# Dilated attention of a three-layer transformer kernel: the order in which eight query tiles are worked on

## Chip, cores and metric

One core of one Trainium2 chip (trn2). The metric is the device time of one execution in microseconds (us), the median of three runs. The profile is of one execution of its own.

## What is computed

The reference runs three layers over 1024 tokens of width 1024 in float32 and returns one array of 1 x 1024 x 1024. The third layer holds the part that matters here: an attention of 8 heads of 64 columns in which a query attends to earlier tokens under three patterns of strides, mixed by their softmax sums.

```
DILATED_CONFIGS = ((128, 1), (512, 4), (2048, 16))      # window, dilation
for window, dilation in DILATED_CONFIGS:
    o, lse = dilated_window_attention(qh, kh, vh, window, dilation)
wts = softmax(stack(lses), axis=0)
o = sum(wts[..., None] * stack(outs), axis=0)           # then * silu(gate)
```

The mixture equals one causal softmax in which each key counts as often as patterns reach it. The kernel computes it so: it adds the logarithm of that count (times 8, or a large negative number where no pattern reaches the key) to the scores, from one table `mask_dilated`.

## The kernel before, in words

The kernel is written out by hand, one instruction stream per engine (TensorE, VectorE, ScalarE, GpSimd, SyncE), joined by semaphores. A planner builds a list of stages once, and each engine's function walks that list. The dilated attention is the stage `att_dil`, kind "dilated"; ahead of it are projections (q, k with their norms, v), behind it the stage "ssm".

The work of the stage is a list of 32 pairs, built at lines 967 to 978: for each query tile `t` of 128 queries (0 to 7) and each head pair `hp` (0 to 3) one pair. Query tile `t` sees the key tiles 0 to `t`, so its score rows are `(t + 1) * 128` keys wide: 128 for tile 0, 1024 for tile 7. `full_pieces` cuts the width into pieces of at most 512 keys, so tiles 0 to 3 have one piece and tiles 4 to 7 two. The two heads of a pair are its two lanes.

`plan_pairs` (line 595) numbers everything in the order of the list: the pair's position `at`, its block (one block per query tile), the PSUM banks of its scores and turned probabilities, and its chunks. A pair's probabilities, `2 * (t + 1)` tiles of 128 x 128 in all, are turned in one chunk (tiles 0 to 3, up to 8 tiles) or in two (tiles 4 to 7: the last 8 in the second one). The score pieces and the first of two chunks take banks in turn from the ring `main` (5 banks), the last chunk of each pair from the ring `turn` (2 banks). A chunk is turned as two halves of 64 rows, one copied out of PSUM by ScalarE and the other by VectorE.

The four loops over the list, one step of each for pair `i` (`u`):

- TensorE (lines 2151 to 2166): scores of pair i+1 (L1705), values of pair i-1 (L2115), turning of pair i (L2087, which waits for both lanes' exponentials of i). Values wait for the chunk's two copies and for the output of the pair before, since all pairs share the PSUM bank of the outputs. After the last pair its values come on their own, then one transpose of the sums (L2170).
- VectorE (lines 3305 to 3323): minima of pair i+1, for each piece both lanes (L3223: adds the mask, scales, stores to SBUF and keeps the minimum), then its half of the copies of pair i (L3237).
- ScalarE (lines 3800 to 3817): exponential of pair i+1, lane 0 (L3718), output of pair i-1 (L3772), its half of the copies of pair i (L3730), exponential of pair i+1, lane 1 (L3718). An exponential works on the whole width of a lane at once and waits for the last minimum of its lane.
- GpSimd (lines 1442 to 1470): when the last pair of a query tile has its output, it stores the tile's block of 128 x 512 to `y_dil` (L1460). Two SBUF blocks alternate (`pair_block`), so a block's first output waits for the store of two blocks before. At the end the inverted sums are stored (L1466), and the stage "ssm" starts its loads (L1542 and on).

Score rows live in one of three SBUF slots per lane (`pair_slot`, by `at % 3`). Sums and outputs are addressed by `t` and `hp`, not by the position in the list. Two further attentions of the kernel use the same loops: the grid attention (2 or 3 local key tiles and 2 of the context, ends at about 1518 us) and, with a loop of its own, the latent attention (1280 keys, starts at about 1034 us).

Of the kernel before, what the change touches and what calls it, by code (L numbers as in the profile page):

```python
# [114 lines left out]
def build(nc, io, out):  # L115
    x, ctx_in = io["x"][0], io["ctx"][0]
    ctx = ExitStack()
    with ctx:
# [651 lines left out]
        with_ctx, tokens = list(range(NTC)), list(range(NT))  # L770
# [42 lines left out]
        def full_pieces(k0, w):  # L813
            return [{"at": at, "k0": k0 + at, "w": min(512, w - at), "add": None} for at in range(0, w, 512)]
# [150 lines left out]
            q["rows"]["after"] = (q["rows"]["ready"] - 1) % 2  # L965
        mask_dilated = RM[:, 0:1024]
        pairs = []
        for t in tokens:
            for hp in range(4):
                w, m0 = (t + 1) * P, (7 - t) * P  # L970
                pieces = full_pieces(0, w)
                for pc in pieces:
                    pc["add"] = mask_dilated[:, m0 + pc["at"]:m0 + pc["at"] + pc["w"]]
                pairs.append({"t": t, "hp": hp, "first": hp == 0, "last": hp == 3, "pieces": pieces,
                              "key_tiles": list(range(t + 1)),
                              "qk": [[(qT[64 * a:64 * a + 64, hp, t * P:(t + 1) * P], kT[64 * a:64 * a + 64, hp, :])
                                      for a in range(2)]],
                              "v": vl, "vc": [128 * hp, 128 * hp + 64], "y": 128 * hp, "to": y_dil[:, :, t * P:(t + 1) * P]})
# [2924 lines left out]
```

How the kernel before makes its waits and increments, by code:

```python
    def wait_full(self, eng, f):  # L100
        eng.wait_ge(self.full, f + 1)
# [1 line left out]
    def wait_drained(self, eng, f):  # L104
        eng.wait_ge(self.drained[self.side[f]], self.count[f])
# [1 line left out]
    def written(self, ins):  # L108
        ins.then_inc(self.full, 1)
# [214 lines left out]
        def wait_weights(eng, n):  # L324
            eng.wait_ge(s_w[weights[n]["slot"]], 16 * weights[n]["loads"] * (weights[n]["nth"] + 1))
# [755 lines left out]
        def wait_x(eng, i):  # L1081
            eng.wait_ge(s_x[i % 4], 16 * (i // 4 + 1))
# [184 lines left out]
        @block.sync  # L1268
        def _(sp):
            row = lambda ap, n: ap.rearrange("(a n) -> a n", a=1).broadcast_to([P, n])
            for n in range(n_weights):
                w = weights[n]
                if w["before"] is not None:
                    (early if w["before"] in even_cols["w"] else main).wait_full(sp, weights[w["before"]]["last"])
                if n == even_rows["w"][0]:
                    sp.wait_ge(s_xn, last_norm + 1)
                    sp.dma_start(bada_row[0], row(io["ev_b_ada"][0][2048:3072], 1024)).then_inc(s_bada, 16)
                if n == odd_rows["w"][0]:
                    main.wait_drained(sp, last_window_scores)
# [16 lines left out]
                j = ple["tiles"][i]  # L1296
                half = slice(512 * c, 512 * c + 512)
                sp.wait_ge(s_ple, n + 1)
                sp.dma_start(out[0, j["t"] * P:(j["t"] + 1) * P, half], x_slot(j["x"])[:, half]).then_inc(s_final[i % 4], 16)
            for r in range(4):
                sp.wait_ge(s_final[r], 32 * len(range(r, len(ple["tiles"]), 4)))
```

## Time and profile before

| | |
|---|---|
| median of 3 runs | 2467.17 us (2466.59 to 2469.29) |
| the profiled execution | 2466.88 us |
| its span, first to last instruction | 2465.1 us |
| instructions | 39768 |
| TensorE matmul busy | 2431.7 us (99%) |
| TensorE weight load busy | 1811.3 us (73%) |
| VectorE busy | 1493.4 us (61%) |
| ScalarE busy | 789.8 us (32%) |
| GpSimd busy | 302.0 us (12%) |
| granted TensorE clock, mean | 1.000 |

The span is the profiled time from the first to the last instruction; 1.8 us lie around it. Busy times of TensorE are those of overlapping matmuls with modelled ends, so a group's duration can reach a little into the next group; from the start of one group to the start of the next is the surer measure. "<-" at an idle time names what ended it.

### The profile page before, as it was taken

What the parts mean: (1) busy time and instruction counts of PE and PEld (TensorE: products, weight loads), DVE (VectorE), ACT (ScalarE), POOL (GpSimd) and SP (SyncE); (2) the same over time, 40 slices, a digit from 0 to 9 for tenths busy, and PEclk for the clock granted to TensorE, in tenths of its full rate; (3) what the DMA queues carried; (4) which work ended last, traced back from release to release, by engine and by line L of the source; (5) the groups of instructions that cost most, each with busy time, mean ns of one, the idle gap of its engine ahead of it and who ended that gap; (6) DMA issues with size and microseconds to landing.
All of it is one profiled execution on the core that took longest, in us unless ns stands there. A gap on an engine that the chain in (4) does not pass through costs nothing.

```text
span 2465.1 us, 39768 instructions
## 1 busy us (share of the span) xinstructions
PE 2431.7 (99%) x15379; PEld 1811.3 (73%) x15379; DVE 1493.4 (61%) x3624; ACT 789.8 (32%) x1849; POOL 302.0 (12%) x491
## 2 busy tenths in 40 slices
PE   9999999999999999999999999999999999999999
PEld 4577688777788785577788776868578775546867
DVE  3268776699776664444452487767778683425454
ACT  3247410377711123333300075112312373221211
POOL 2001000000051000000060042310000004132100
PEclk9999999999999999999999999999999999999999
DMA  8130010122032220311011013432241206244421
GB/s 300 43 108 24 19 35 35 43 75 78 18 119 96 89 91 30 107 44 43 14 24 40 34 60 37 123 108 99 90 150 35 78 19 166 98 139 151 154 77 51
DMA packets 79498, 193.74 MB, mean 79 GB/s; under 512 B 7948, under 2 KB 18896, under 8 KB 78272
## 3 DMA queue, kind: packets, MB, share of 16 engines
q0 software_dynamic: 28928, 99.67, 12.9%
q1 hardware_dynamic: 49632, 91.17, 10.7%
q8 instruction: 123, 2.02, 0.3%
q14 instruction: 63, 0.52, 0.1%
q10 hardware_dynamic: 752, 0.38, 0.1%
HBM read 149.46 MB, written 42.07 MB: 78 GB/s over the span
## 4 chain that ended last, share of the span: by engine, by line
PE 95%; DVE 2%; ACT 1%; issue 1%; DMA 1%; DVEq 0%; SPq 0%; POOL 0%; ACTq 0%
PE psum L1672 38%; PE psum L1705 12%; PE psum L2007 8%; PE psum L2118 6%; PE psum L2115 5%; PE psum L2199 4%; PE psum L2087 4%; PE psum L1811 3%; PE psum L1928 3%; PE psum L1658 1%; PE psum L1639 1%; PE psum L2273 1%; PE psum L2291 1%; PE psum L2257 1%; PE psum L1980 1%
## 5 line engine op out<-in xcount | busy, mean ns | idle before, releaser
L3718 ACT ACTIVATE RP<-RP,small 128x1280 f32<-128x1280 f32 (+10 forms) x272 | 250.4, 923 | 183.4 <-DVE small L3223 183.0
L1705 PE MATMUL psum<-RQ 64*128 64x256 f32 (+5 forms) x1344 | 287.7, 488 | 1.7 <-ACT RQ L3460 0.8
L3223 DVE CUSTOM_DVE_ANT_0 RP<-psum,small 128x512 f32<-128x512 f32 (+1 forms) x370 | 197.2, 571 | 58.9 <-PE psum L1705 54.8
L2007 PE MATMUL psum<-RW,hT 128*128 128x512 f32 (+3 forms) x608 | 217.1, 512 | 1.0 <-ACT hT L3426 1.0
L1705 PEld LDWEIGHTS psum<-RQ 64*128 64x128 f32 (+1 forms) x1344 | 147.4, 188 | 82.3 <-issue 55.1
L2007 PEld LDWEIGHTS psum<-RW,hT 128*128 128x128 f32 x608 | 128.8, 217 | 75.4 <-issue 57.8
L1672 PE MATMUL psum<-RW,hT 128*128 128x256 f32 x736 | 167.1, 379 | 0.0
L1672 PEld LDWEIGHTS psum<-RW,hT 128*128 128x128 f32 x736 | 139.7, 190 | 22.2 <-issue 2.1
L1672 PE MATMUL psum<-RW,RP 128*128 128x256 f32 x576 | 136.2, 379 | 0.0
L2115 PEld LDWEIGHTS psum<-RP,RQ 128*64 128x64 f32 x1856 | 100.3, 137 | 46.2 <-issue 30.4
L2115 PE MATMUL psum<-RP,RQ 128*64 128x128 f32 x1856 | 124.5, 278 | 7.8 <-DVE RP L3237 4.2
L2118 PE MATMUL psum<-RQ,RP 128*128 128x128 f32 x1024 | 125.5, 279 | 0.8 <-DVE RP L3245 0.8
L2087 PEld LDWEIGHTS psum<-ident,RP 64*128 64x128 f32 x2668 | 97.0, 139 | 39.0 <-issue 27.1
L2118 PEld LDWEIGHTS psum<-RQ,RP 128*128 128x128 f32 x1024 | 119.2, 192 | 4.1 <-DVE YR L3279 0.9
L2087 PE MATMUL psum<-ident,RP 64*128 64x64 f32 x2668 | 112.4, 227 | 6.3 <-ACT RP L3718 5.5
L1672 PEld LDWEIGHTS psum<-RW,RP 128*128 128x128 f32 x576 | 107.7, 190 | 13.4
L3237 DVE COPY RP<-psum 128x512 f32<-128x512 f32 (+3 forms) x168 | 87.6, 525 | 35.8 <-PE psum L2087 33.3
L1672 PE MATMUL psum<-RW,RQ 128*128 128x256 f32 x480 | 108.9, 379 | 0.0
L1672 PEld LDWEIGHTS psum<-RW,RQ 128*128 128x128 f32 x480 | 90.5, 190 | 12.6 <-issue 1.0
L1672 PE MATMUL psum<-RQ,RP 128*128 128x256 f32 x432 | 97.2, 380 | 0.9 <-issue 0.9
L1672 PEld LDWEIGHTS psum<-RQ,RP 128*128 128x128 f32 x432 | 81.6, 190 | 11.9 <-issue 1.3
L1811 PE MATMUL psum<-RW,hT 128*128 128x512 f32 x160 | 73.7, 595 | 0.6 <-DVE hT L2562 0.6
(574 smaller groups left out, 4249.7 us busy)
## 6 DMA issues: line engine op xcount, KB each, us to landing
RW<-in_w_in SPq DMA_DIRECT2D x7, 2048.0 KB, 7.9
RW<-in_od_w_ada SPq DMA_DIRECT2D x6, 2048.0 KB, 8.2
RW<-in_ev_w_in SPq DMA_DIRECT2D x5, 2048.0 KB, 7.9
RW<-in_od_w_in SPq DMA_DIRECT2D x5, 2048.0 KB, 7.8
RQ<-in_ev_w_ada SPq DMA_DIRECT2D x8, 1024.0 KB, 14.9
RX<-in_x POOLq DMA_DIRECT2D x12, 512.0 KB, 7.4
RW<-in_ev_w_ada SPq DMA_DIRECT2D x2, 2048.0 KB, 8.6
RW<-in_ev_w_out SPq DMA_DIRECT2D x2, 2048.0 KB, 9.0
```

What stands on the lines that cost most here:

```text
L1672: last = pe.matmul(main.bank(f)[:, 0:256], lhs(i), rhs[:, i, :], start=i == 0, stop=i == 3)
L1705: last = pe.matmul(ring.bank(f)[:, 0:pc["w"]], q, kk[:, keys], start=i == 0, stop=i == len(u["qk"]) - 1)
L1811: return pe.matmul(main.bank(j["m"]), lhs_of("h", j["t"], kk), w_buf(n)[:, kk, :], start=kk == 0, stop=kk == KC - 1)
L1928: last = pe.matmul(main.bank(f), yT[kk], w_buf(st["w"][c])[:, kk, :], start=kk == 0, stop=kk == KC - 1)
L2007: last = pe.matmul(main.bank(f)[:, c0:c0 + nc_], lhs_of(st["lhs"], j["t"], kk), w, start=kk == 0, stop=kk == kn - 1)
L2087: last = pe.transpose(ring.bank(f)[:, HD * i:HD * i + HD], pair_slot(st, u, lane)[rows, at:at + P], ident[rows, rows])
L2115: last = pe.matmul(bank_o[64 * lane:64 * lane + 64, 0:P], u["v"][:, kt, vc:vc + 64], p_t, start=first, stop=final)
L2118: last = pe.matmul(bank_o[:, P * lane:P * lane + P], p_t, u["v"][:, kt, vc:vc + P], start=first, stop=final)
L2199: last = pe.matmul(main.bank(e["m"]), *pair, start=kk == 0, stop=kk == KC - 1)
L3223: drained(ring, dve.tensor_tensor_reduce(pair_slot(st, u, lane)[:, pc["at"]:pc["at"] + pc["w"]], ring.bank(f)[:, 0:pc["w"]], add, -scale, ...
L3237: drained(ring, dve.tensor_copy(turned_half(ch, 1), src), f)
L3718: fn(pr, pr, ACT.Exp, bias=mins[:, at, lane, n - 1:n], scale=-1.0, accum_out=total).then_inc(s_pexp, 1)
```

## The change

The list of pairs is built over the query tiles in another order. The head pairs inside a tile, and everything that is computed for a pair, stay as they are.

```diff
@@ -965,7 +965,7 @@
             q["rows"]["after"] = (q["rows"]["ready"] - 1) % 2
         mask_dilated = RM[:, 0:1024]
         pairs = []
-        for t in tokens:
+        for t in (5, 0, 6, 1, 7, 2, 4, 3):
             for hp in range(4):
                 w, m0 = (t + 1) * P, (7 - t) * P
                 pieces = full_pieces(0, w)
```

`tokens` is 0 to 7. All engines take the new order, since all walk the same list.

## Rows read from the trace of the kernel before

**Rows 1.** The page: engines' share of the span, and the chain by engine

```profile
PE 2431.7 (99%) x15379; PEld 1811.3 (73%) x15379; DVE 1493.4 (61%) x3624; ACT 789.8 (32%) x1849; POOL 302.0 (12%) x491
...
PE 95%; DVE 2%; ACT 1%; issue 1%; DMA 1%; DVEq 0%; SPq 0%; POOL 0%; ACTq 0%
```

**Rows 2.** Busy time by stretch: length, engines (instructions), clock, DMA share, GB/s

```profile
1951.86:2049.40 97.54, 93.34 (x1345) 66.64 (x1345) 77.12 (x242) 75.36 (x207) 5.00 (x7) 1.00 0.13 43
...
1958.50:1965.50 7.00, 6.36 (x76) 3.73 (x76) 4.93 (x20) 6.13 (x26) 0.74 (x1) 1.00 0.21 66
...
2031.00:2049.50 18.50, 17.71 (x303) 14.20 (x302) 12.98 (x33) 12.24 (x26) 0.71 (x1) 1.00 0.06 17
```

**Rows 3.** Timeline of the stage's first steps, tile 0: start, duration, what, [idle before]

```profile
1951.86 0.71 PE L1705 MATMUL psum<-RQ 64*128 64x128 f32 x8
...
1953.25 0.39 ACT L3718 ACTIVATE RP<-RP,small 128x128 f32<-128x128 f32 x1
...
1953.78 0.34 PE L2087 MATMUL psum<-ident,RP 64*128 64x64 f32 x4 [1.21 <-ACT RP L3718]
...
1956.55 0.26 ACT L3772 ACTIVATE YR<-psum 128x128 f32<-128x128 f32 x1
...
1956.70 0.27 ACT L3730 ACTIVATE RP<-psum 128x128 f32<-128x128 f32 x1
...
1956.86 0.40 ACT L3718 ACTIVATE RP<-RP,small 128x128 f32<-128x128 f32 x1
```

**Rows 4.** Timeline, TensorE's gaps where the next tile is one longer

```profile
1958.73 0.44 PE L2115 MATMUL psum<-RP,RQ 128*64 128x128 f32 x4 [0.42 <-ACT RP L3730]
...
1965.69 0.66 PE L2115 MATMUL psum<-RP,RQ 128*64 128x128 f32 x8 [0.30 <-ACT RP L3730]
...
1985.60 1.10 PE L2115 MATMUL psum<-RP,RQ 128*64 128x128 f32 x16 [0.41 <-issue]
```

**Rows 5.** Timeline, TensorE's gaps at the stage's end, tile 7

```profile
2043.98 1.97 PE L2115 MATMUL psum<-RP,RQ 128*64 128x128 f32 x32 [0.39 <-DVE RP L3237]
...
2047.50 1.97 PE L2115 MATMUL psum<-RP,RQ 128*64 128x128 f32 x32 [0.40 <-DVE RP L3237]
```

**Rows 6.** Timeline, TensorE: one step of tile 5, then scores of 6 and 7

```profile
2004.53 1.51 PE L1705 MATMUL psum<-RQ 64*128 64x512 f32 x8
...
2005.96 1.53 PE L2115 MATMUL psum<-RP,RQ 128*64 128x128 f32 x24
...
2007.42 0.96 PE L2087 MATMUL psum<-ident,RP 64*128 64x64 f32 x24
...
2008.22 1.72 PE L1705 MATMUL psum<-RQ 64*128 64x512 f32 x8
...
2029.18 1.93 PE L1705 MATMUL psum<-RQ 64*128 64x512 f32 x8
```

**Rows 7.** Timeline, first exponentials of tiles 4 (with its scores), 5, 6 and 7

```profile
1987.30 1.30 PE L1705 MATMUL psum<-RQ 64*128 64x512 f32 x8
...
1990.14 0.83 ACT L3718 ACTIVATE RP<-RP,small 128x640 f32<-128x640 f32 x1 [0.86 <-DVE small L3223]
...
2007.50 0.94 ACT L3718 ACTIVATE RX<-RX,small 128x768 f32<-128x768 f32 x1 [0.84 <-DVE small L3223]
...
2011.33 1.05 ACT L3718 ACTIVATE RP<-RP,small 128x896 f32<-128x896 f32 x1 [0.97 <-DVE small L3223]
...
2032.42 1.15 ACT L3718 ACTIVATE RX<-RX,small 128x1024 f32<-128x1024 f32 x1 [1.08 <-DVE small L3223]
```

**Rows 8.** Timeline of other attentions: latent, first turning; grid, last values

```profile
1040.23 0.71 PE L2087 MATMUL psum<-ident,RP 64*128 64x64 f32 x16 [1.99 <-ACT RP L3718]
...
1517.23 1.09 PE L2115 MATMUL psum<-RP,RQ 128*64 128x128 f32 x16 [0.91 <-DVE RP L3237]
```

**Rows 9.** DMA issues of 1940 to 2080 us: KB each, median us to landing

```profile
y_dil<-YR POOLq DMA_DIRECT2D x8, 256.0 KB, 2.7
```

**Rows 10.** Busy time by stretch around the latent attention's start, clock third from last

```profile
1036.00:1060.00 24.00, 21.38 (x170) 14.56 (x169) 11.51 (x34) 8.42 (x14) 0.00 (x0) 1.00 0.28 102
```

## The prediction, made before the change was run

> **What bounds the kernel now.** I read the page first: TensorE is busy for 99% of the span and makes up 95% of the chain of waits that ended last [rows 1], so a change is worth what it adds to or takes from TensorE's path. Next the stretches: the dilated attention lasts 97.5 us, 4.0% of the span, with TensorE busy for 93.34 us of it, VectorE for 77.12 and ScalarE for 75.36 [rows 2]. TensorE still ends most waits, but in the short tiles it is not full (6.36 of 7.00 us), and in the last stretch it isn't either. Then the timeline, where the gaps lie: 1.21 us before the first turning, small ones at the short tiles and on the way into tile 4, two at the end [rows 3 to 5].
>
> **How one step is built.** Every engine walks the same list of 32 pairs (8 tiles, 4 head pairs). In step i TensorE computes the scores of pair i+1, then the values of pair i-1, then turns (transposes) pair i. VectorE runs the masked minima of i+1 and then half of the copies of i. ScalarE runs the exponential of i+1's lane 0, the output of i-1, its half of the copies of i, the exponential of i+1's lane 1. So between the scores of a pair and its turning stand only the values and the turning of the two pairs before it. With neighbours of like length these cover the minima and exponentials; with a short pair ahead of a long one they don't.
>
> **What is removed or added: nothing.** The same 32 pairs with the same widths run on each engine: no instruction, byte or DMA more. Only seams between tiles and both ends of the stage change. Before, the seams go up by one tile seven times. After, they go down four times (5 to 0, 6 to 1, 7 to 2, 4 to 3) and up three times by a lot (0 to 6, 1 to 7, 2 to 4); the stage starts with tile 5 instead of 0 and ends with 3 instead of 7.
>
> **Prices, start to start.** In tile 5 scores take 1.43 us (2004.53 to 2005.96), values 1.46, turning 0.80 [rows 6]. A tile of 128 keys more or less is 0.21 in scores (1.93 against 1.51 over two tiles), 0.22 in values (1.97 against 1.53) and 0.13 in turning (0.96 against 0.34 over five) [rows 3, 5, 6]. Four steps of each of the eight tiles make 91.7 us, against 97.5 measured: 5.8 us of stall, 4.2 of it visible as gaps [rows 2], the rest as stretched groups of scores or values. The other half of a seam is how late the first exponential comes after the start of the scores: 2.84 us in tile 4, 2.97 in tile 5, 3.11 in tile 6, 3.24 in tile 7; one then lasts 0.83, 0.94, 1.05 and 1.15 us [rows 6, 7]. On ScalarE an output takes 0.15 us and the copy of a pair of tile 0 0.16 (1956.55, 1956.70, 1956.86) [rows 3]; a tile more adds 0.1 to a copy, as it does to an exponential. The turning follows the end of the second by 0.14 (1953.25 plus 0.39, then 1953.78) [rows 3].
>
> **The start.** Tile 5: first exponential at 2.97, two of 0.94, turning at 5.0 us. TensorE has two scores of 1.43 to do meanwhile, 2.86 us: it stalls 2.1. Tile 0 stalls 1.21 [rows 3]. Extra 0.9. Bounds: nothing extra, and 1.3 (a cold start twice as wide, with 1280 keys, idles 1.99 [rows 8]; 2.1 is already beyond it, and 0.4 is for a slower bank).
>
> **5, 0, 6.** Going down, the values of the last pair of tile 5 come right behind 0.37 us of scores, where 1.43 covered its copies: about 0.2, and the turning before it waits 0.35 for its lane 1 exponential (which in a row of tile 5 pairs has 1.43 us of scores ahead of it, here 0.37). Inside tile 0 the steps stay bound by the handing back and forth, as now. Going up, count from the start of the scores of the first pair of tile 6. Its exponential starts at 3.11 and ends at 4.16; behind it on ScalarE stand the output of the pair before last and the copy of the last pair of tile 0, until 4.5; then lane 1 until 5.5, turning at 5.65. TensorE has scores 1.66, values 0.37, turning 0.17, scores 1.66, so it is through at 3.9; the last values of tile 0 can start at 4.65 (a stall of 0.8), end at 5.0, and the turning waits 0.65 more. With the 0.6 that two steps of tile 0 lose inside, this makes 2.6 us. Tile 0 and its way into tile 1 lose 1.3 today (gaps like the 0.42 ahead of the last of them [rows 4], and stretched groups). Extra 1.3.
>
> **6, 1, 7.** Same walk: exponential at 3.24 to 4.4, output and copy to 4.8, lane 1 to 5.95, turning at 6.1; TensorE is through with scores 1.86, values 0.59, turning 0.29, scores 1.86 at 4.6: 0.35, then 0.55; inside tile 1 0.45, a bank 0.15. 1.5 against 0.8 today. Extra 0.7.
>
> **7, 2, 4, 3.** Exponential at 2.84 to 3.7, output and copy to 4.2, lane 1 to 5.0; TensorE is through at 3.7: 0.65; inside tile 2 0.25. 0.9 against 0.4. Extra 0.5. On the other side the seam from 3 to 4, now a gap of 0.41 and a little stretch [rows 4], and a part of tile 4's stretched groups go: minus 0.65 together.
>
> **The end.** The last two values wait for copies with no scores in between. Tile 7's pairs are turned in two chunks, the first is copied while the second is turned: 0.39 and 0.40 us [rows 5]. A pair of tile 3 is one chunk of 16 transposes, and the grid attention ends with exactly such a pair: 0.91 [rows 8]. Twice 0.91 less 0.79: extra 1.0, the firmest term.
>
> **What costs nothing.** The block stores land 2.7 us after issue [rows 9], and their buffer is wanted again two tiles later; the shortest tile in between lasts over 4 us (four steps of 0.9 and their stalls). If that cover were gone, the price would be 2.7 once. The next stage starts from the end of this one whatever the tile, so a delay passes on in full.
>
> **Sum.** 0.9 + 1.3 + 0.7 + 0.5 - 0.65 + 1.0 = 3.75, taken as 3.8 us. Bounds: if the three upward seams cost no more than now, the sum is 1.3 (0.9, -0.65, 1.0); if each costs as much as the cold start (2.1), it is 7.1. I take the walked value, since its durations are rows of this stage and its end is a row of a like stage. The profiled execution took 2466.88 us, 0.3 below the median of 2467.17: it would take 2470.7, the median 2471.0. About 0.2%, 4.9 us, is what a measurement can tell from no change.
>
> **Rivals.**
>
> *The seams cost as much as the start (slower).* Place: ScalarE's queue at the three upward seams. The long exponential stands ahead of an output and a copy that the values of the short pair need, and the five score banks may hold back the second long pair as well. For it: in the cold start TensorE finds nothing to do, and a pair of tile 0 offers it only 0.9 us of work. Against: the scores of a second long pair, 1.2 to 1.9 us, lie in the seam. Price: 0.9 + 1.0 + 3 x 2.1 - 1.2 (today's seams into 1, 2 and 4: 0.42, 0.30 and 0.48 [rows 4]) = 7.1, so 2474.3. It decides from 1.8 us a seam. Chance 0.2.
>
> *Short and long tiles fill each other (no loss, slightly faster).* For it: in the tiles 0 to 2 TensorE isn't full, while in tile 7 it has 17.71 us of work in 18.50 [rows 2]. If the order removed the 2.5 us that these three tiles lose, and the seams cost nothing: 0.9 + 1.0 - 0.65 - 2.5 = -1.2, so 2466.0. Against: four steps of a short tile still follow each other, and only the first and the last of them touch a long one. Chance 0.15. The Trainium skill (Perfetto Trace Analysis, Optimization Strategy) says that a kernel whose most contended engine changes from stretch to stretch may gain from interleaving the stretches; by that rule the time comes out on this side. The trace so far agrees that the stretches differ, not that tiles are fine enough a grain.
>
> *The clock falls in a longer gap.* The granted clock is 1.00, the higher of its two levels, also in the stretch that holds the 1.99 us idle of the cold start at 1040 us [rows 10]; the longest gap that I expect is 2.1. If it fell to the lower of its two levels, 1.2 GHz, for the work of one long tile, 17.71 us [rows 2] would double: 2485. Chance 0.02. The Trainium skill (TensorE: Matmul & The Clock Gate, HAM oscillation) warns that a wait which leaves the array idle can bring the next matmuls at half rate; the rows here show no such fall.
>
> **How the numbers follow.** Forecast 0.63, slower seams 0.2, filling 0.15, clock 0.02. Of the forecast some 0.08 lies beyond 4.9 us (its own spread is about 1.5 to either side); with 0.18 of the slower seams and 0.02 of the clock that is 0.28 for slower. Faster would take a gain of 4.9 us, most of the 5.8 that the stage stalls at all: 0.03, out of the filling case. 0.69 is left for the same. The range takes the sum from 0.3 to 7.1: 2467.5 to 2474.3, which holds the forecast and the slower seams and leaves out most of the filling case and the clock.
>
> **What would show it.** Right: a stage of about 101.3 us; the first turning after an idle of 1.9 to 2.2; gaps of 0.5 to 0.9 ahead of the last values of tiles 0, 1 and 2 and ahead of the first turning of tiles 6, 7 and 4; two gaps of 0.9 at the end; busy times and counts as before; nothing moved outside the stage. Wrong: a stage of under 98.5 us (then a short pair's values cover more than I counted) or over 104 (then the seam spreads into further steps, seen as stretched scores of the second and third long pair), or a granted clock below 1.00.

## The result, and the profile after

| | before | after |
|---|---|---|
| median of 18 runs of each | 2469.24 us (2466.59 to 2473.26) | 2473.24 us (2471.04 to 2475.89) |
| ratio after to before | | 1.0014 (1.0008 to 1.0020), +3.5 us |
| profiled execution, span | 2465.1 us | 2473.7 us |
| stage of the dilated attention | 97.54 us | 101.61 us |
| forecast | | 2471.0 us (2467.5 to 2474.3), stage 101.3 us |

The new order costs a little, 0.14%, less than the 0.2% set in the prediction as what can be told from no change. With 18 executions instead of three, the median of the kernel before stands 2.1 us above the one shown ahead; that is nearly the whole of the 2.2 us by which 2473.24 lies above the forecast. (The two medians differ by 4.0 us; the 3.5 is what the ratio makes of 2469.24.) One of all the executions in this document, of "before_filled" below, took 2799.57 us, in a slow state, and is left out of that kernel's ratio and spread. A page of the profile can't show a thing of this size. These are its engines and its chain ([rows 1] has the same two lines of before):

```profile
PE 2437.5 (99%) x15379; PEld 1811.0 (73%) x15379; DVE 1495.8 (60%) x3624; ACT 791.9 (32%) x1849; POOL 302.5 (12%) x491
...
PE 91%; issue 2%; DVE 2%; ACT 2%; DMA 2%; POOL 1%; DVEq 0%; SPq 0%; POOLq 0%; ACTq 0%
```

All counts are those of before, as they must be when the same pairs are run. The view by stretches, with the columns of [rows 2], shows where it lies, first the stage, then the stretch around the latent attention's start:

```profile
1956.13:2057.74 101.61, 94.61 (x1345) 66.72 (x1344) 76.69 (x242) 76.75 (x207) 5.02 (x7) 1.00 0.13 41
1036.00:1060.00 24.00, 21.41 (x161) 14.43 (x161) 11.13 (x33) 8.43 (x14) 0.00 (x0) 0.86 0.31 113
```

The stage is 4.07 us longer than in [rows 2], at full clock, with VectorE 0.4 us less and ScalarE 1.4 us more busy, and TensorE 1.27 us busier (longer groups of scores, of which more below). That is the change. But the span grew by 8.6 us. Of the other 4.5 us, 4.27 had come before the stage began (1956.13 against 1951.86), in stages that the change doesn't touch; the largest part is in the second row: a granted clock of 0.86 where [rows 10] has 1.00. TensorE alone, in four windows of it (length, busy, clock, DMA share, GB/s):

```profile
1036.00:1040.00 4.00, 3.08 (x10) 1.00 1.05 389
1040.00:1044.00 4.00, 2.33 (x42) 0.70 0.77 283
1044.00:1048.00 4.00, 4.00 (x12) 0.50 0.02 4
1048.00:1052.00 4.00, 4.00 (x11) 0.95 0.00 0
```

The clock fell from its higher level to 0.50, which is 1.2 GHz, right behind the idle time ahead of the latent attention's first turning (1.99 us in both kernels), and was back soon after 1048 us. TensorE ran 0.84 us behind the kernel before at that turning and 3.67 us behind it afterwards: 2.8 us, which are no part of the change. The rest of the 4.27 isn't a matter of the clock: 0.84 had come before that turning, and about 0.7 comes near 1810 us, where an idle time lasts 1.27 us in place of 0.59 (1.01 in "start5", 0.90 in "seams"); why it varies wasn't traced. Falls are not bound to one order: the mean clocks of the executions of the kernel before lie between 0.997 and 1.000, and "latent_filled" below shows one in the order 0 to 7. So orders are compared by the length of their stage.

### The profile page after: what moved, and what is told of

Same layout as the page of the kernel before. It is cut to its first block, busy times and chain, and to the rows that moved or that the text cites. A ratio compares the mean times of both kernels' runs of the same rounds, so it can differ in the third digit from the quotient of the medians.

```text
span 2473.7 us, 39768 instructions
## 1 busy us (share of the span) xinstructions
PE 2437.5 (99%) x15379; PEld 1811.0 (73%) x15379; DVE 1495.8 (60%) x3624; ACT 791.9 (32%) x1849; POOL 302.5 (12%) x491
## 3 DMA queue, kind: packets, MB, share of 16 engines
q0 software_dynamic: 28928, 99.67, 12.8%
## 4 chain that ended last, share of the span: by engine, by line
PE 91%; issue 2%; DVE 2%; ACT 2%; DMA 2%; POOL 1%; DVEq 0%; SPq 0%; POOLq 0%; ACTq 0%
PE psum L1672 37%; PE psum L1705 12%; PE psum L2007 8%; PE psum L2118 6%; PE psum L2115 5%; PE psum L2087 4%; PE psum L2199 3%; PE psum L1811 3%; PE psum L1928 2%; PE psum L1658 1%; PE psum L1639 1%; PE psum L2273 1%; PE psum L2291 1%; PE psum L1980 1%; PE psum L1759 1%
## 5 line engine op out<-in xcount | busy, mean ns | idle before, releaser
L1672 PE MATMUL psum<-RQ,RP 128*128 128x256 f32 x432 | 97.2, 379 | 0.9 <-issue 0.9
L3730 ACT ACTIVATE RP<-psum 128x512 f32<-128x512 f32 (+3 forms) x168 | 71.3, 459 | 9.7 <-PE psum L2087 8.9
```

The costliest lines, as they stand in the source:

```text
L1672: last = pe.matmul(main.bank(f)[:, 0:256], lhs(i), rhs[:, i, :], start=i == 0, stop=i == 3)
L3730: ring.consumed(fn(turned_half(ch, 0), src, ACT.Copy), f)
```

## The seams, one by one

The timeline of after on TensorE (start, duration, what, idle before), at the stage's start and from tile 5 down into tile 0 and up to tile 6:

```profile
1956.13 3.76 PE L1705 MATMUL psum<-RQ 64*128 64x512 f32 x16
1961.18 0.97 PE L2087 MATMUL psum<-ident,RP 64*128 64x64 f32 x24 [1.28 <-DVE small L3223]
...
1970.22 1.54 PE L2115 MATMUL psum<-RP,RQ 128*64 128x128 f32 x24 [0.40 <-ACT RP L3730]
...
1977.19 1.72 PE L1705 MATMUL psum<-RQ 64*128 64x512 f32 x8
...
1979.38 1.84 PE L1705 MATMUL psum<-RQ 64*128 64x512 f32 x8
1981.86 0.44 PE L2115 MATMUL psum<-RP,RQ 128*64 128x128 f32 x4 [0.64 <-ACT RP L3730]
1982.84 1.09 PE L2087 MATMUL psum<-ident,RX 64*128 64x64 f32 x28 [0.54 <-ACT RX L3718]
```

The first turning starts 5.05 us after the stage does. The gap of 1.28 us before it looks like the 1.21 of [rows 3], and yet the start lost 1.0 us more: the two groups of scores before it last 3.76 us where two of 1.43 would do. Within them the weight loads of the second pair's scores wait for VectorE's minima, whose end frees the score banks:

```profile
1958.18 0.29 PEld L1705 LDWEIGHTS psum<-RQ 64*128 64x128 f32 x2 [0.47 <-DVE small L3223]
1958.79 0.70 PEld L1705 LDWEIGHTS psum<-RQ 64*128 64x128 f32 x4 [0.32 <-DVE small L3223]
```

A gap is only what is left when the group ahead of it has been stretched; start-to-start times tell the loss. At the upward seam the scores of tile 6 begin at 1977.19; the last values of tile 0 come 4.67 us after that and the turning 5.65 us. Who releases them is ScalarE, whose own timeline is:

```profile
1980.30 1.04 ACT L3718 ACTIVATE RX<-RX,small 128x896 f32<-128x896 f32 x1 [2.19 <-DVE small L3223]
1981.34 0.26 ACT L3772 ACTIVATE YR<-psum 128x128 f32<-128x128 f32 x1
1981.49 0.27 ACT L3730 ACTIVATE RP<-psum 128x128 f32<-128x128 f32 x1
1981.65 1.04 ACT L3718 ACTIVATE RX<-RX,small 128x896 f32<-128x896 f32 x1
```

The long exponential, an output, the copy that the short pair's values need, the second exponential: a queue in order, walked in the prediction, 3.11 us behind the scores as forecast. The seams into tiles 7 and 4, and the end of the stage:

```profile
2006.46 0.66 PE L2115 MATMUL psum<-RP,RQ 128*64 128x128 f32 x8 [0.33 <-ACT RP L3730]
2007.55 1.22 PE L2087 MATMUL psum<-ident,RP 64*128 64x64 f32 x32 [0.42 <-ACT RP L3718]
...
2033.95 0.88 PE L2115 MATMUL psum<-RP,RQ 128*64 128x128 f32 x12 [0.64 <-ACT RP L3730]
...
2054.07 1.09 PE L2115 MATMUL psum<-RP,RQ 128*64 128x128 f32 x16 [0.90 <-DVE RP L3237]
...
2056.72 1.09 PE L2115 MATMUL psum<-RP,RQ 128*64 128x128 f32 x16 [0.91 <-DVE RP L3237]
```

The gaps at these seams are smaller than the prediction's sign asked for (0.5 to 0.9 at all six places): 0.33 and 0.42 us at tile 7, and none ahead of the first turning of tile 4, where all of the loss lies in the 0.64 ahead of the values. The last two are the gaps of 0.91 that the prediction took from a like pair [rows 8], in place of 0.39 and 0.40 [rows 5].

## Experiments

The theory (S, the seams and ends) says that the cost is made of four separate places and adds up. Against it stand: the order itself, through buffers and rings that were tuned for 0 to 7 (D); the interleaving of unlike pairs as a gain that only lacks a finer grain (C); and the clock (F). Each profile's stage is measured from its first scores to the transpose that follows its last values. The whole times say little here, since the seven kernels that change the order or ScalarE's queue ran once each: "start5" 2471.44, "end3" 2472.05, "seams" 2470.49 and "descending" 2471.05 us beside one execution of the kernel before of 2468.37; "copies_first" 2473.82 and "by_pairs" 2479.66 beside its median of 2469.03; "copies_first_2" 2470.15 beside 2470.45. In "copies_first" 2.4 us of it lie behind the stage (418.1 us from there to the end, in place of 415.7), at a mean clock of 1.00.

### Parts of the order alone

The edit is to the same line as the change, in the kernel before. "start5":

```
-        for t in tokens:
+        for t in (5, 0, 1, 2, 3, 4, 6, 7):
```

> Order 5, 0, 1, 2, 3, 4, 6, 7: the start and the first downward seam of the change alone; the end is tile 7 again. The stage took 97.5 us before and 101.6 after. Theory A (each seam costs what ScalarE's queue leaves uncovered): start +0.9, seam 5 to 0 +0.7 (as in the profile after), seam 4 to 6 no more than today's two seams of one tile: 99.1 us, 98.7 to 99.5. Rival B (any jump up costs as much as a cold start, 2.1): the seam 4 to 6 adds 2 more: 101. Rival C (a short tile fills what a long one leaves): under 97.5.

Measured: stage 99.25 us, against 99.1 expected. The part alone costs about what it costs in the sum. "end3":

```
-        for t in tokens:
+        for t in (0, 1, 2, 4, 5, 6, 7, 3):
```

> Order 0, 1, 2, 4, 5, 6, 7, 3: the end of the change alone, with one upward seam of two tiles (2 to 4). Theory A: two gaps of 0.91 in place of 0.39 and 0.40, so +1.0; seam 2 to 4 0.65 against 0.6 to 0.7 in today's seams 2 to 3 to 4; seam 7 to 3 up to 0.2: 98.7 us, 98.4 to 99.0. Rival B: +1.0 and +1.4 for the seam 2 to 4: 100. Rival C: the short tile behind tile 7 is filled, 97.5 to 98.

Measured: stage 100.55 us, 1.9 above what S expected. TensorE in two windows of it, then two places of its timeline:

```profile
1957.00:1959.00 2.00, 2.00 (x20) 0.50 1.05 409
1959.00:1961.00 2.00, 2.00 (x18) 0.50 1.01 382
```

```profile
1955.81 0.34 PE L2087 MATMUL psum<-ident,RP 64*128 64x64 f32 x4 [1.21 <-ACT RP L3718]
...
2050.76 1.09 PE L2115 MATMUL psum<-RP,RQ 128*64 128x128 f32 x16 [0.91 <-DVE RP L3237]
```

The clock was at its lower level in these 4 us, behind the start's own gap of 1.21 us. This kernel's first two tiles are those of the kernel before, so the two can be laid side by side: the same transposes of tile 1 start 10.78 us after the stage instead of 9.00. Without these 1.78 us the stage is 98.8, as S expected, and its end has the 0.91. "seams":

```
-        for t in tokens:
+        for t in (0, 5, 1, 6, 2, 4, 3, 7):
```

> Order 0, 5, 1, 6, 2, 4, 3, 7: the start and end of the kernel before, the jumps of the change between them, four of them up. Theory A: 0 to 5 1.5, 1 to 6 1.0, 2 to 4 0.65, 3 to 7 nothing, 0.5 to 0.7 for the seams down, and what tiles 0 to 2 lose inside: 99.6 us, 99.0 to 100.2. Rival B (2.1 for each upward jump): 104. Rival C: under 97.5.

Measured: stage 99.67 us against 99.6, with both ends as before:

```profile
1962.05 0.44 PE L2115 MATMUL psum<-RP,RQ 128*64 128x128 f32 x4 [0.74 <-ACT RP L3730]
1962.91 0.96 PE L2087 MATMUL psum<-ident,RP 64*128 64x64 f32 x24 [0.43 <-ACT RP L3718]
...
1985.72 1.09 PE L2087 MATMUL psum<-ident,RP 64*128 64x64 f32 x28 [0.32 <-ACT RP L3718]
...
2010.21 0.88 PE L2115 MATMUL psum<-RP,RQ 128*64 128x128 f32 x12 [0.65 <-ACT RP L3730]
```

One pair of gaps for each step up by five tiles; going up by two costs the values alone 0.65. The seam from 3 to 7 shows no gap at all ahead of the values of tile 3, but isn't free, as S had it: the scores of the third pair of tile 7 take 2.28 us from start to start, where 1.86 is usual. "descending":

```
-        for t in tokens:
+        for t in (7, 6, 5, 4, 3, 2, 1, 0):
```

> Order 7 to 0: no upward seam at all. Theory A: start with tile 7 stalls 2.0 (+0.8), the end with tile 0 stalls 0.73 twice (+0.35), the seams of today (1.5 us in all) go: 97.2 us, 96.7 to 97.8, about as before. Rival B (starts and jumps are what counts, at 2.1 each): the same sign, 97 to 98, so this run doesn't part A from B; it parts both from rival D, that the order of the bank rings or the POOL stores is what costs: then any order other than 0 to 7 is longer, 99 or more.

Measured: stage 100.47 us, not 97.2. A fall of the clock at its start (0.50 for 2 us, with 0.77 and 0.88 around it) accounts for an estimated 1.6, from what the same instructions last at full clock in the other profiles. The other 1.7 is a miss of S, which priced a step down by one tile at nothing:

```profile
2029.46 1.09 PE L2115 MATMUL psum<-RP,RQ 128*64 128x128 f32 x16 [0.20 <-DVE RP L3237]
...
2038.82 0.88 PE L2115 MATMUL psum<-RP,RQ 128*64 128x128 f32 x12 [0.29 <-DVE RP L3237]
...
2046.27 0.66 PE L2115 MATMUL psum<-RP,RQ 128*64 128x128 f32 x8 [0.36 <-DVE RP L3237]
```

Each of these stands twice at its seam. The values of the last two long pairs wait for copies that the scores of the pair two ahead used to cover, and those scores have become shorter. From start to start such a step loses 0.5 us from 3 to 2, 0.7 from 2 to 1 and 0.9 from 1 to 0, but 0.1 or less between longer tiles. Steps up by one tile aren't free either [rows 4], but of all the orders run, 0 to 7 has the shortest stage. By the marks set ahead of it this run doesn't part S from D: 98.9 us without the fall is nearer to D's "99 or more" than to 97.2. Against D speak the traces. In no stage of the orders run does TensorE, VectorE or ScalarE wait for GpSimd or a DMA, so the stores cost nothing. Banks do hold scores back, at the start and in the third long pair, but as a part of a seam; a cost of the order as such, apart from ends and seams, isn't seen.

### Pair by pair

If unlike pairs filled each other's gaps (C), alternating them singly should do better than four by four. "by_pairs" alternates 5 with 0, 6 with 1, 7 with 2 and 4 with 3 for each head pair; the block number is kept per tile, as the blocks are open side by side.

```
-        for t in (5, 0, 6, 1, 7, 2, 4, 3):
-            for hp in range(4):
+        for long, short in ((5, 0), (6, 1), (7, 2), (4, 3)):
+            for t, hp in [(t, hp) for hp in range(4) for t in (long, short)]:
```

> The grain made as fine as it goes: tiles 5 and 0, 6 and 1, 7 and 2, 4 and 3 alternate pair by pair (head pair 0 of the long one, of the short one, head pair 1, ...). Theory A: each of the 16 long pairs now comes behind a short one and pays an upward seam, by the walk 1.5 (5, 0), 1.0 (6, 1), 0.4 (7, 2) and 0.4 us (4, 3) each: 91.5 + 13 + 3 for start and end = 107.5 us, 106 to 109. Rival C (interleaving long and short fills the gaps, only the grain was too coarse): under 101.6, at best under 97.5.

Measured: stage 109.96 us, which is above the range of S; 1.65 of it is a fall of the clock at its start, and the 108.3 without it lie inside. Its second step up, from tile 0 to tile 5:

```profile
1969.21 0.44 PE L2117 MATMUL psum<-RP,RQ 128*64 128x128 f32 x4 [0.92 <-ACT RP L3732]
1970.07 0.97 PE L2089 MATMUL psum<-ident,RP 64*128 64x64 f32 x24 [0.43 <-ACT RP L3720]
```

So a finer grain makes it worse, 10.8 us for 15 steps up and the two ends, against 4.1 for three steps up and the same ends. The pipeline is two pairs deep and ties each pair's values and turning to its neighbours' scores, whatever tile they belong to.

### ScalarE's queue at a seam

If the order of ScalarE's queue makes the upward seam dear, another order there should make it cheaper. "copies_first" is the kernel after, with the long exponential behind the output and the copies, only where the next pair is longer:

```
-                            for nxt in ps[i + 1:i + 2]:
+                            late = k == "dilated" and i + 1 < len(ps) and ps[i + 1]["w"] > u["w"]
+                            for nxt in () if late else ps[i + 1:i + 2]:
                                 exponential(nxt, 0)
...
                             turned_chunks(u, u["turns"])
+                            for nxt in ps[i + 1:i + 2] if late else ():
+                                exponential(nxt, 0)
```

> The changed order, and in the three steps whose next pair belongs to a longer tile (0 to 6, 1 to 7, 2 to 4) ScalarE does the output and the copy ahead of the exponential of lane 0 instead of behind it. Theory A (the last short pair's values wait for them in ScalarE's queue, and lane 1's exponential too): 0.3 less at 0 to 6, 0.4 at 1 to 7, 0.3 at 2 to 4; the gap ahead of the last values of the short tile goes (0.64, 0.33, 0.64 in the profile after), the one ahead of the turning grows in part: stage 100.6 us, 100.3 to 100.9. Rival B (banks or VectorE hold the seam): 101.6, gaps as before.

Measured: stage 101.46 us, not 100.6: the length that B expected, but not with B's gaps.

```profile
1978.81 1.09 PE L2087 MATMUL psum<-ident,RX 64*128 64x64 f32 x28 [0.92 <-ACT RX L3718]
1979.74 1.99 PE L1705 MATMUL psum<-RQ 64*128 64x512 f32 x8
1981.66 1.75 PE L2115 MATMUL psum<-RP,RQ 128*64 128x128 f32 x28
```

The turning did move up (5.32 us behind the start of the seam's scores, from 5.65; 5.67 from 6.10 and 4.81 from 5.21 at the other two), so the queue does set it. But 0.3 to 0.4 us was lost again at each in the next group of scores, at the first 1.92 us from start to start where 1.65 is usual. The suspect was a PSUM bank for the third long pair's scores, which comes free with the copy of the first long pair's first chunk, now queued behind an exponential. Where a wait goes must be followed one step further. "copies_first_2" gives that chunk its place back, in the step after the seam:

```
+                            first_long = k == "dilated" and i and u["w"] > ps[i - 1]["w"] and len(u["turns"]) > 1
+                            if first_long:
+                                turned_chunks(u, u["turns"][:1])
```

> copies_first moved the turning of the first long pair up by 0.33, 0.43 and 0.40 us and lost 0.27, 0.44 and 0.30 again in the scores of the third long pair, whose last piece waits for the bank of the first pair's first chunk, which ScalarE copies only behind the exponential of the second pair. Here that copy is put ahead of this exponential too, in the same three places. If the bank is the cause: the groups of scores behind the first turning of tiles 6, 7 and 4 are back to 1.65, 1.86 and 1.23 us and the stage takes 100.5 us (100.2 to 100.8). If the seam is bound by VectorE's minima instead, the loss shows one step later and the stage stays at 101.4.

Measured: stage 100.39 us, against 100.5 expected, and the group of scores behind the first turning is back at 1.65 us (1978.93 to 1980.58), and at the other two seams at 1.87 and 1.23, which shows the bank:

```profile
1978.00 1.09 PE L2087 MATMUL psum<-ident,RX 64*128 64x64 f32 x28 [0.92 <-ACT RX L3718]
1978.93 1.72 PE L1705 MATMUL psum<-RQ 64*128 64x512 f32 x8
1980.58 1.75 PE L2115 MATMUL psum<-RP,RQ 128*64 128x128 f32 x28
```

1.2 of the 4.1 us are given back by ScalarE's order alone. It is no better than the order 0 to 7.

### The clock, and filling TensorE's gaps

The falls were first seen in the kernel after, so F says that its time is, in part, a matter of the clock. "before_filled" puts products of the identity, into a PSUM bank that is free then, into the two idle times, in the kernel before: 8 calls (16 instructions in the trace) ahead of the latent attention's first turning, 5 ahead of the dilated one's.

```
+            def fill_gap(n):
+                for _ in range(n):
+                    pe.matmul(bank_o[:, 0:P], ident[:, :], ident[:, :], start=True, stop=True)
...
+                            elif k == "dilated":
+                                fill_gap(5)
...
+                    fill_gap(8)
```

> The kernel before (order 0 to 7) with matmuls on the identity put into two gaps of TensorE, their result is overwritten later: 8 of 128x128 into the 1.99 us ahead of the latent attention's first turning, 5 into the 1.21 us ahead of the dilated attention's. In three of five traces so far the granted clock fell to 0.5 in the first, in two of five right behind the second, at 3.4 and 1.8 us each time. Theory A (the idle lets the clock fall): clock 1.00 in both stretches, median 1 to 3 us under the kernel before, smaller spread of the runs; the dilated stage 97.5 us in the profile. Rival E (the falls come by themselves, filled or not): the same median within 0.5 us, falls still seen in the profile.

(Two slips in that text: the traces that it counts as five were six, and the fall that it puts at 3.4 us is the 2.8 above.) Measured: median 2466.67 us of 11 runs against 2469.03 for the kernel before, ratio 0.9987 (0.9978 to 0.9996). Its stretches in the columns of [rows 2] and [rows 10], and the places that were filled:

```profile
1950.98:2048.57 97.59, 94.59 (x1356) 67.80 (x1355) 77.11 (x242) 75.36 (x207) 5.01 (x7) 1.00 0.13 43
1036.00:1060.00 24.00, 23.16 (x186) 16.56 (x185) 11.49 (x34) 8.43 (x14) 0.00 (x0) 1.00 0.28 104
```

```profile
1038.27 1.95 PE L1780 MATMUL psum<-ident 128*128 128x128 f32 x16
1040.42 0.71 PE L2092 MATMUL psum<-ident,RP 64*128 64x64 f32 x16 [0.21 <-ACT RP L3726]
...
1951.62 1.38 PE L1780 MATMUL psum<-ident 128*128 128x128 f32 x10
1952.94 0.34 PE L2092 MATMUL psum<-ident,RP 64*128 64x64 f32 x4
```

The stage is no shorter (97.59); what is gained is gained where the clock would have fallen. Ten of its runs spread over 2.2 us, the 21 of the kernel before beside them over 6.9. The filling doesn't rule falls out: one of the ten, of 2467.97 us, has a mean clock of 0.998. "after_filled" does the same to the kernel after, with 9 calls in the dilated gap:

> The changed kernel with the same filling: 8 ahead of the latent attention's first turning, 9 ahead of the dilated attention's (a stall of 2.1 us). Theory A: without falls of the clock what is left between this and before_filled is the stage's own 4.1 us: ratio of the two 1.0016 to 1.0018, stage 101.6 us in the profile. Rival E: as before_filled. Rival F (part of the 3.5 us measured is a clock that falls more often behind the longer gap): the difference of the filled pair is under 3 us.

Measured: 2471.36 us, ratio to before 1.0010 (1.0001 to 1.0019), but with a stage of 102.47 us: nine calls were too many. The pair of filled kernels, timed in one set, differs by 2471.36 - 2466.67 = 4.7 us, 3.8 without the 0.86 by which the filling lengthened the stage. Rival F wanted under 3.

```profile
1954.57 2.27 PE L1780 MATMUL psum<-ident 128*128 128x128 f32 x18
1956.77 0.96 PE L2092 MATMUL psum<-ident,RP 64*128 64x64 f32 x24
```

They held the turning up until 5.90 us after the start, instead of 5.05. The same with five calls, "after_filled_5":

```
-                                fill_gap(9)
+                                fill_gap(5)
```

> after_filled had 9 matmuls in the dilated attention's first gap; they took 2.27 us and ended 0.85 us after the turning could have started (turning at 5.90 us from the stage's start, 5.05 without them), so its stage was 102.5 us. Here 5 of them, 1.2 us, which end in time. Theory A: stage 101.6 us in the profile, median 4.0 us (3.6 to 4.4) above before_filled's 2466.7, so 2470.7; spread of the runs about 1 us as there. Rival F (a clock fall is still behind a part of it): the runs spread over 3 us or more, with lows at 2470.7.

Measured: 2470.91 us, beside 2470.45 for the kernel before in the same set (ratio 1.0002, 0.9992 to 1.0011). The stage row is that of after but for the filling:

```profile
1950.82:2052.43 101.61, 95.91 (x1355) 67.94 (x1354) 76.70 (x242) 76.75 (x207) 5.02 (x7) 1.00 0.13 41
```

With both kernels filled, the new order costs 2470.91 - 2466.67 = 4.2 us, and 101.61 - 97.59 = 4.0 of it is the stage. The two were timed in different sets, in which the kernel before differed by 1.4 us, so 4.2 is good to a microsecond or two; the 3.8 above, from one set, agrees. The runs of "after_filled_5" spread over 2.6 us, between the 1 of theory A and the 3 of F, and three of the eleven lie under 2470.7. F falls by the times: where the clock hardly moves, the order costs as much. "latent_filled" is the kernel before with the first of the two fillings alone:

```
+                    fill_gap(8)
```

> The kernel before with the filling in the latent attention alone (8 matmuls). Parts the 2.4 us that before_filled gained. Theory A: most falls come behind the 1.99 us gap and cost 3.4 us each, so this keeps 1.5 to 2.2 us of the gain; the runs are at 2466.7 or, where the clock falls behind the dilated attention's start, 1.8 us above. Rival: all of the gain comes from the dilated attention's start, then this is within 0.5 us of the kernel before.

Measured: 2468.35 us against 2470.45, ratio 0.9990 (0.9981 to 0.9999), 2.1 us gained. Its profile caught the other fall, behind the unfilled gap of the dilated attention; TensorE in four windows:

```profile
1954.00:1956.00 2.00, 2.00 (x21) 0.55 1.05 409
1956.00:1958.00 2.00, 2.00 (x16) 0.50 1.00 378
1958.00:1960.00 2.00, 2.00 (x18) 0.50 0.05 14
1960.00:1962.00 2.00, 2.00 (x27) 0.74 0.03 10
```

Its stage lasted 99.53 us instead of 97.54. So both places matter, each in some executions. How much of the 2.4 us of "before_filled" belongs to which is not settled; the intervals of the two kernels overlap.

## Why the prediction was right

The forecast was no measurable change, with a cost of 3.8 us; measured were 3.5 (2.0 to 4.9) in time and 4.07 in the stage. The difference is what it got right. That 2473.24 us also lies in the range is owed in part to the range's width, as the three executions that it started from were 2.1 us faster than the median of 18.

| step of the prediction | forecast, us | shown, us |
|---|---|---|
| first turning, from the stage's start | 5.0 | 5.05 |
| start, extra | +0.9 | +1.0 |
| 5, 0, 6: stalls in all | 2.6 | 2.8 |
| last values of tile 0, first turning of 6 | 4.65, 5.65 | 4.67, 5.65 |
| 6, 1, 7: stalls; first turning of 7 | 1.5; 6.1 | 1.5; 6.10 |
| 7, 2, 4: stalls; first turning of 4 | 0.9; 5.1 | 1.0; 5.21 |
| two gaps at the end | 0.91 each | 0.90, 0.91 |
| stage | 101.3 | 101.61 |

- **The start.** Right in size; its form was not. The forecast awaited an idle time of 1.9 to 2.2 us; the trace shows 1.28, and the rest as stretched scores.
- **Down from 5 to 0.** Under-sized by 0.2 (0.55 forecast; 0.47 and 0.27 shown). "The turning before it waits 0.35 for its lane 1 exponential" is the step that failed: the wait lies ahead of the values of the last pair but one (0.40, released by ScalarE's copy), since one short group of scores covers the copies there.
- **Up.** The walk through ScalarE's queue held to 0.07 us at all three seams. It is also what "copies_first" and its successor moved.
- **Downward by one, 4 to 3.** The prediction counted only a gain there (the step from 3 to 4 that goes). Stepping down by one costs something as well: 0.5 to 0.9 us between short tiles in "descending", but less than 0.1 here from 4 to 3. The 0.3 us between 3.75 and 4.07 lie at the start (0.1) and around tile 0 (0.2).
- **The end.** Right; "end3" shows it alone.
- **What costs nothing.** Busy times on VectorE, ScalarE and GpSimd in the stage are those of before within 1.4 us, and from the stage's end to the last instruction it is 415.96 us, from 415.70.
- **"Nothing moved outside the stage".** Wrong for the profiled execution, by 4.27 us, of which the fall of the clock is 2.8. The rest, some 0.7 of it near 1810 us, wasn't traced to a cause.
- **The rivals.** Seams as dear as the cold start: refuted (0.7 to 1.4 us at the step up itself, not 2.1). Its price was added up wrong by a little: the terms give 7.0, not 7.1. Filling each other: refuted by the stage, and by pairs even more. The prediction put the rule of the Trainium skill (Perfetto Trace Analysis, Optimization Strategy) beside it, that interleaving stretches with different bounds may gain; in this stage it went the other way, +4.1 us by tiles and +10.8 by pairs, which the tie between neighbours in one in-order pipeline would explain.
- **The clock.** The prediction took its single profile without a fall [rows 10] as a sign that gaps of this length do no harm, gave 0.02 and a price of 17.7 us. Falls are common and cheap: 1.3 to 2.8 us each. Its sign of being wrong, a granted clock below 1.00, did show, in a stage that the change doesn't touch. That falls leave the difference between the kernels alone is no more than what the filled pair shows: 3.8 us in one set, against 3.5.

## What to carry to other kernels

In a software pipeline whose stages lean on the neighbouring item, try first an order in which items of unlike size grow by small steps, which starts with the smallest and ends with one whose last copies can overlap its own work (here the shortest of seven orders); to price another order, walk the slowest in-order queue at each jump, beginning with the start of the long item's first operation. Read losses from start to start, since a gap may be hidden in a stretched group. Where totals scatter by more than the effect, compare the stage's length, and look at the granted clock first.

## What the runs showed of the hardware that was not expected

**A short idle time of TensorE may be followed by the lower clock, in the same kernel sometimes and sometimes not.** The latent attention's gap of 1.99 us stood unfilled in nine profiled executions; in three of them (of the kernels after, "end3" and "descending") the granted clock fell behind it, to 0.50 where it was looked at closely, which cost 2.8, 1.7 and 1.3 us. The dilated attention's first gap stood unfilled in ten; in four (1.21, 1.28, 1.21 and 2.51 us idle) the clock fell, for 1.6 to 2.0 us of lost time, while gaps of 1.21, 1.28 and 1.29 us left it at 1.00 in others. Where the gaps were filled, in four and three executions, it never fell there. At the rate of the unfilled ones, 7 in 19, seven without a fall would come by chance about once in 25 (an estimate), so the traces alone are thin; the gain in time of both kernels with the order 0 to 7 that were filled stands beside them. The Trainium skill (TensorE: Matmul & The Clock Gate, HAM oscillation) warns of a wait that brings the next matmuls at half rate; the traces agree (0.50 for several us), and add that here it is a matter of chance and can be bought off: 13 idle products of the identity gave 2.4 us of 2469.

**The two gaps are not the only places.** In "start5" the clock fell near 150 us, behind two idle times of 0.76 and 0.78 us that stand in all thirteen profiled executions, unfilled; the other twelve have 1.00 there. From the turning that follows to the next but one it took 9.16 us, where the kernel before takes 7.16.

```profile
150.00:152.00 2.00, 2.00 (x15) 0.72 1.03 396
152.00:154.00 2.00, 1.71 (x19) 0.50 1.05 403
```

**Filling has its own edge.** Ten instructions of it fit the idle time (1.38 us, stage unchanged at 101.61); eighteen (2.27 us) held the turning up by 0.85 us, and the stage grew by 0.86.
